# First attention layer with its queries in reverse order inside each block of 128, so that the bias table loads straight from its short form

## The reference, cut to what matters

```
q = rms_norm(proj[..., :o1].reshape(b, s, 16, 64), q_gain)
score = where(admissible, sum_h w[t,h] * relu(q_idx[t,h] . k_idx[s]), NEG)
_, idx = top_k(score, 64)
logits = einsum(q, k[idx]) * 64 ** -0.5 + rel_bias[t5_bucket(idx - t)]
p = softmax(where(valid, logits, NEG))
out = einsum(p, v[idx]) @ w_o
```

## Time and profile before

| | |
|---|---|
| median of 3 runs | 1142.5 us (1140.87 to 1145.25) |
| the profiled execution, its own time | 1142.08 us |
| its span, first to last instruction | 1140.3 us |
| mean granted TensorE clock | 0.994 of full |
| TensorE busy | 1114.7 us, 98% of the span |
| VectorE, ScalarE, GpSimd busy | 709.4, 583.4, 147.4 us |
| memory read, written | 191.90 MB, 6.37 MB |

### The profile page before, as it was taken

One profiled execution on the slowest core, in us unless ns is written; L12 is line 12 of the kernel. 1 busy time (PEld: TensorE's weight loads), 2 busy tenths in 40 slices (PEclk: granted clock), 3 DMA queues, 4 the chain that ended last, 5 costly groups with the idle time before them and its releaser, 6 DMA issues.

```text
span 1140.3 us, 17804 instructions
## 1 busy us (share of the span) xinstructions
PE 1114.7 (98%) x7045; PEld 987.8 (87%) x7045; DVE 709.4 (62%) x995; ACT 583.4 (51%) x767; POOL 147.4 (13%) x106
## 2 busy tenths in 40 slices
PE   8999999999999999999999999999999999999997
PEld 7768788888888888888888999898899989999996
DVE  5863665655668656556556877476587655554554
ACT  5583644444679554444455546445546346443443
POOL 3544200000266330000030000000000022000001
PEclk9999999999999999999999999999999999999999
DMA  7927465565342246555554655336554444655552
GB/s 224 313 70 180 160 221 185 185 191 190 112 138 104 74 137 227 190 185 184 188 180 162 209 152 182 114 122 238 177 166 132 165 150 152 220 180 194 189 172 89
DMA packets 138782, 193.96 MB, mean 170 GB/s; under 512 B 7147, under 2 KB 112840, under 8 KB 138716
## 3 DMA queue, kind: packets, MB, share of 16 engines
q1 hardware_dynamic: 126796, 181.92, 48.7%
q10 hardware_dynamic: 11312, 11.05, 3.6%
q0 software_dynamic: 608, 0.08, 0.1%
HBM read 191.90 MB, written 6.37 MB: 174 GB/s over the span
## 4 chain that ended last, share of the span: by engine, by line
PE 84%; DVE 6%; ACT 4%; DMA 2%; issue 2%; POOL 1%; SPq 0%; ACTq 0%; DVEq 0%
PE psum L546 20%; PE psum L547 20%; PE psum L548 20%; PE psum L707 11%; PE psum L708 5%; PE psum L635 2%; ACT arena L1553 2%; ACT whi L1567 1%; POOL wlo L1536 1%; DVE psum L2496 1%; DMA raw<-in_a_w_in 1%; DMA raw<-in_mlp_w_up 1%; PE psum L1265 1%; DVE wlo L2124 1%; DVE arena L2326 1%
## 5 line engine op out<-in xcount | busy, mean ns | idle before, releaser
L1567 ACT ACTIVATE whi<-raw 128x2048 fp32r<-128x2048 f32 (+2 forms) x174 | 325.8, 1874 | 260.8 <-PE psum L548 161.9
L2124 DVE TENSOR_TENSOR wlo<-raw,whi 128x2048 fp32r<-128x2048 f32 (+1 forms) x148 | 337.8, 2284 | 187.3 <-ACT whi L1567 186.4
L546 PE MATMUL psum<-xA,whi 128*128 128x256 f32 x840 | 240.1, 286 | 3.0 <-POOL wlo L1536 2.0
L547 PE MATMUL psum<-xA,whi 128*128 128x256 f32 x840 | 237.7, 283 | 0.0
L548 PE MATMUL psum<-xA,wlo 128*128 128x256 f32 x840 | 237.7, 283 | 0.0
L1536 POOL TENSOR_TENSOR wlo<-raw,whi 128x288 fp32r<-128x288 f32 (+3 forms) x57 | 117.3, 2083 | 803.6 <-ACT whi L1567 803.5
L707 PE MATMUL psum<-xA,whi 128*128 128x512 f32 x512 | 182.9, 400 | 0.8 <-DVE xA L2150 0.8
L546 PEld LDWEIGHTS psum<-xA,whi 128*128 128x128 f32 x840 | 160.7, 191 | 6.4 <-DVE wlo L2124 2.2
L547 PEld LDWEIGHTS psum<-xA,whi 128*128 128x128 f32 x840 | 160.7, 191 | 0.7
L548 PEld LDWEIGHTS psum<-xA,wlo 128*128 128x128 f32 x840 | 160.6, 191 | 0.1
L546 PE MATMUL psum<-whi,xC 128*128 128x512 f32 (+1 forms) x384 | 149.7, 390 | 1.1 <-DVE xC L2436 1.1
(11 more groups left out here) (272 smaller groups left out, 1344.0 us busy)
## 6 DMA issues: line engine op xcount, KB each, us to landing
raw<-in_w_in SPq DMA_DIRECT2D x42, 1024.0 KB, 5.0
raw<-in_mlp_w_up SPq DMA_DIRECT2D x32, 1024.0 KB, 5.5
raw<-in_mlp_w_down SPq DMA_DIRECT2D x32, 1024.0 KB, 4.9
raw<-in_w_gate SPq DMA_DIRECT2D x11, 1024.0 KB, 5.2
raw<-in_w_up SPq DMA_DIRECT2D x11, 1024.0 KB, 5.2
raw<-in_w_down SPq DMA_DIRECT2D x11, 1024.0 KB, 4.9
raw<-in_a_w_in SPq DMA_DIRECT2D x6, 1024.0 KB, 7.2
raw<-in_a_w_o SPq DMA_DIRECT2D x4, 1024.0 KB, 5.2
```

Source lines behind the costliest of these rows:

```text
L546: nc.tensor.matmul(out, lh, rh, start=start, stop=False, skip_group_check=skip)
L547: nc.tensor.matmul(out, lh, rl, start=False, stop=False, skip_group_check=skip)
L1567: nc.scalar.activation(whi[c % N_SPLIT][:, 0:n], raw[c % N_RAW][:, 0:n], ACT.Copy).then_inc(hi_sem, 1)
L2124: V.tensor_tensor(wlo[c % N_SPLIT][:, 0:n], raw[c % N_RAW][:, 0:n], f(whi[c % N_SPLIT][:, 0:n]), ALU.subtract).then_inc(lo_sem["dve"], 1)
```

## The change

The transposes of the queries use a matrix `flip` (the identity with its rows reversed) in the place of the identity, so that query 127 of a block comes first. Row r of the logits then is query 127 - r, and its bias is the line of the head from place r on: `A["toep"]` loads directly from `tab_a` with rows that start one value later each (`falling_rows`), and `skew_a` with its transfer is gone. The mask is brought into the same order by using the bf16 `flip` in its product, and the transposes of the attention's output use `flip` again, which restores the order. `flip` is loaded as one more constant, the first of the eleven behind `q0b`; its bf16 copy is made by DVE between the scores and the picking, behind a wait for all constants. TensorE waits for the constants ahead of the first query transposes. The third layer keeps its own path.

```
-        const_loads = [(relb[:, 16:40], t["rel_bias_2"]), ...
+        const_loads = [(flip[:, :], t["c_flip"]), (relb[:, 16:40], t["rel_bias_2"]), ...
...
-            def transposed(name, b, tiles):
+            def transposed(name, b, tiles, unit=ident):
...
-                    ins = nc.tensor.transpose(out[0:m, n * P:n * P + P], src, ident[:, :])
+                    ins = nc.tensor.transpose(out[0:m, n * P:n * P + P], src, unit[:, :])
...
                 pe.wait_ge(*done[f"A.qn{j}"])
+                if j == 0:
+                    pe.wait_ge(s_const, 16 * N_CONST)
                 for i, b in enumerate(banks):
                     transposed(f"A.qT{2 * j + i}", b, [A["q"][:, blk, k * P:k * P + P]
-                                                       for k in (4 * j + 2 * i, 4 * j + 2 * i + 1) for blk in range(NB)])
+                                                       for k in (4 * j + 2 * i, 4 * j + 2 * i + 1) for blk in range(NB)], flip)
...
-                        ins = nc.tensor.matmul(psum[:, logit_bank[h % 4], c0:c0 + w], ident_bf[:, :],
+                        ins = nc.tensor.matmul(psum[:, logit_bank[h % 4], c0:c0 + w], flip_bf[:, :],
                                                pick_mask[:, blk, 0:w], start=False, stop=True)
...
+            def falling_rows(tab, n):
+                return bass.AP(tab.ap().tensor, 0, [[1, P], [512, n], [1, SEQ]])
...
-            act.wait_ge(s_tab, 16)
-            shift_rows(tab_a, skew_a, 16)
...
-            act.wait_ge(s_skew, 16)
-            act.dma_start(A["toep"], skew_a.ap().rearrange("h p s -> p h s")).then_inc(s_toep_a, 16)
+            act.wait_ge(s_tab, 16)
+            act.dma_start(A["toep"], falling_rows(tab_a, 16)).then_inc(s_toep_a, 16)
...
-            run(V.tensor_copy(ident_bf[:, :], ident[:, :]), done["A.ident"])
+            run(V.tensor_copy(ident_bf[:, :], ident[:, :]))
...
+            dve.wait_ge(s_const, 16 * N_CONST)
+            run(V.tensor_copy(flip_bf[:, :], flip[:, :]), done["A.ident"])
```

More of the change, by code:

```diff
@@ L103, in shape_constants @@
         pick[h, h * P:(h + 1) * P] = 1.0
-    return {"c_ident": np.eye(P, dtype=np.float32), "c_one_a": one_a, "c_one_c": one_c, "c_off_c": off_c,
+    return {"c_ident": np.eye(P, dtype=np.float32), "c_flip": np.ascontiguousarray(np.eye(P, dtype=np.float32)[::-1]),
+            "c_one_a": one_a, "c_one_c": one_c, "c_off_c": off_c,
             "c_rope": rope, "c_turn": np.ascontiguousarray(turn), "c_chunk_mask": chunk_mask.astype(np.float32),
@@ L130, in program @@
         ident_bf = sb("ident_bf", [P, P], BF16)
+        flip = sb("flip", [P, P])
+        flip_bf = sb("flip_bf", [P, P], BF16)
         chunk_mask = sb("chunk_mask", [P, P], BF16)
@@ L143, in program @@
         tab_c = nc.dram_tensor("tab_c", (24, 512), F32, kind="Internal")
-        skew_a = nc.dram_tensor("skew_a", (16, P, SEQ), F32, kind="Internal")
         skew_c = nc.dram_tensor("skew_c", (24, P, SEQ), F32, kind="Internal")
@@ L492, in program @@
         tab_loads = [(relb[:, 0:16], t["rel_bias"]), (one_hot_a, t["c_one_a"])]
-        const_loads = [(relb[:, 16:40], t["rel_bias_2"]), (one_hot_c, t["c_one_c"]), (off_c, t["c_off_c"]),
+        const_loads = [(flip[:, :], t["c_flip"]), (relb[:, 16:40], t["rel_bias_2"]), (one_hot_c, t["c_one_c"]), (off_c, t["c_off_c"]),
                        (casts[:, 0, :], t["c_chunk_mask"]), (casts[:, 1, :], t["c_later"]),
@@ L774, in out_turned @@
                     transposed(f"{L}.oT{g}", g % 2, [S["o"][:, g, blk * 256 + i * P:blk * 256 + i * P + P]
-                                                     for i in range(2) for blk in range(NB)])
+                                                     for i in range(2) for blk in range(NB)], flip if L == "A" else ident)
                 def product(j, quarters):
@@ L1998, in _ @@
                     done[f"C.ya{k // 2}.hi"] if k % 2 else None, scale=vec(V_ML + k))
-            act.wait_ge(s_skew, 32)
+            act.wait_ge(s_skew, 16)
             for h in range(2):
```

## The result

The changed kernel takes 1149.97 us (median of 12 executions, 1147.18 to 1152.39) against 1144.95 us of the kernel before (12 executions, 1140.87 to 1150.53): a ratio of 1.0041, 95% interval 1.0021 to 1.0061. It is 5.0 us slower, and 1149.97 is outside the predicted range of 1139.2 to 1144.4. Of the 8.3 us between the forecast of 1141.7 and the result, 2.5 are in the kernel before, whose median over 12 executions is that much above the 1142.5 of its first three; the other 5.8 are a loss of 5.0 where a gain of 0.8 was forecast. The loss is 0.44%, so it still falls into the case "within 0.5%" that got 0.92, but its interval reaches beyond that. The profiled execution took 1151.51 us, with a span of 1149.7.

A forecast was written before the change was run, and what follows sets the result against it. TensorE, busy 98% of the span, bounds the kernel; only its waits can be won. Gains of 0.5 (q0b) and 0.6 (q1a), limited by POOL's scaling to 0.8, give 1141.3, or 1141.7 as median; range 1139.2 to 1144.4.

The forecast's parts named there:

- within 0.5%: Whole kernel: time changes by no more than 0.5% (5.7 us) either way; chance 0.92.
- the new copy of flip: DVE between scores and picking, near 39 us: costs 0.23 us, as the identity's cast did, plus 0.03 between instructions.
- What was late next: First query transposes at 55.89 wait for POOL's scaling, which hangs on DVE; gains there bring the total to 0.8 us.
- The wait for the constants: DVE ahead of flip's cast, about 39 us: priced at nothing, cover over 1 us; bound 1.5 us of wait.
- the signs that the forecast named for being wrong: Constants wait before DVE's cast, wo0 landing after 55, or a query transpose waiting over 0.5 us for POOL.
- The transfers: Without the shift, q1a lands 5.0 to 5.7 us after issue, not 11.1; bias load issued at 38.7, landing by 49.
- dear short form: Rival at the bias load: unaligned packets cost up to 102 ns, wo0 lands near 57.0, total 1143.7; chance 0.15.
- The 0.5 us for q0b: Second dot products at 34.22: q0b lands 0.55 us earlier without the shift, TensorE's wait shrinks from 1.22 to about 0.7.
- the forecast of 0.8: TensorE's total gain by the first query transposes at 55.89, taken from 0.55 to 0.9 us and carried to the end.
- more comes back: Rival at the attention's start: earlier wo0 pulls the first exponentials forward, up to 2 us gained, 1140.5; chance 0.12.
- Slower: Rival for the whole kernel: the bias load from the short form delays wo0, 1143.7; chance 0.15.
- the four cases: Whole kernel: forecast (0.3 to 1.5 us faster) 0.53, hidden anyway 0.2, more comes back 0.12, slow short form 0.15.

The follow-up runs named there:

- the old cast moved: Kernel before, with only the identity's bf16 cast moved from 29.7 us to ahead of the seventh picking turn, beside POOL's work; span 1141.3 us.
- the copy on ACT: Changed kernel with the bf16 copy of flip made by ACT behind the bias load's issue, not by DVE; ratio to before 0.9970, median 1140.98 us.
- the transfers alone: Kernel before without the first layer's shift, bias loaded directly from the short form, no flip (output differs); ratio to before 0.9982.
- flip alone: Kernel with flip copied by ACT, but the bias again through a written 2 MB table and a second load; ratio to before 1.0009.

## Why the prediction was wrong, by its own steps

**The step that failed** is in the sentence that begins "Against it goes the new copy of flip, 0.23 by the same cast of the identity". The row is right and was read without its surroundings. At 29.71 POOL was idle; at 38.5 it had just begun a subtraction, and that by my own sum (POOL from 38.7, DVE's cast "near 39"): the two stood side by side in the forecast, and nothing asked whether they can run together. The term measured 4.52 us. The trace of before showed the effect, in a row that I passed over. DVE's timeline has the same instruction twice, once while POOL's subtractions of 42.84 to 52.05 were under way, once without:

```profile
51.24 0.85 DVE L2302 TENSOR_SCALAR st<-st 128x16 f32<-128x16 f32 x1
...
62.82 0.17 DVE L2302 TENSOR_SCALAR st<-st 128x16 f32<-128x16 f32 x1
```

The first of them ends at 52.09, just behind POOL. The later profiles of before bear it out: in the second it took 1.30 us and ended at 52.91, with POOL's subtraction at 52.88; in the third, where POOL had ended at 53.75, it started at 55.21 and took 0.17. A blocked instruction has no bracket; it is only too long for its shape. The instructions of the picking are not long beside POOL (MAX8 0.29 us with and without it), which is why the picking never showed it.

```profile
51.61 1.30 DVE L2302 TENSOR_SCALAR st<-st 128x16 f32<-128x16 f32 x1
```

The Trainium skill says the same (SBUF — State Buffer, Who interferes with whom): copies, casts and tensor_scalar of DVE in their fast modes, and any DVE instruction with two inputs in SBUF against a GpSimd instruction that reads SBUF, share a port pair with GpSimd, and whoever comes first holds it for its whole instruction. The runs agree: 4.52 for the cast, 4.58 for the product of two SBUF inputs, 1.19 when POOL's instruction is a quarter as long, each ending within 0.2 us of POOL's instruction. That what is shared is a port, no run here can show; they show who waited, and how long. By that rule the term would have been the rest of POOL's 4.6 us.

**What was late next** was named rightly: POOL's scaling and the transposes behind it had 0.28 us of room. With a delay of 4 us in DVE the forecast's own structure gives the first half of the loss. The second half, 2.7 us, was in no step: in TensorE's wait of 3.91 us its clock fell to 1.2 GHz, and the transposes behind it took 1.97 us instead of 1.03.

**The wait for the constants** was priced at nothing, and it was nothing: DVE passed it with no wait. Of the signs that the forecast named for being wrong, the wait for constants did not come and wo0 landed in time; the third, a query transpose that waits over 0.5 us for POOL, did, with 3.91.

**The transfers** were right in mechanism, but not each gain has been seen. q1a landed 5.9 us after its issue, was copied at 36.30 with no wait, and the wait at its first product is gone. The bias load was issued at 36.30, at the start of that copy and not behind it (38.7), and landed at 47.1 (by 49). Its packets cost 1.082 x 16 x 2.4 / 821 = 51 ns each, in the range of 49 to 60 that I took, so the rival of a dear short form (beyond 87 ns) is out; wo0, issued at 42.94, landed 6.7 us later, near 49.6, and was copied at 55.04 and not before 54, because ACT waited for DVE.

The 0.5 us for q0b is not borne out. The changed kernel has its dot products 0.97 earlier than before (33.25 against 34.22), but its clock in the first 20 us was 1.00 and not 0.91. Where the clock there was the same, little is left: with the shift and 1.00, the kernel with the old cast moved has them at 33.42 and its key transposes at 45.98 (45.79 in the changed kernel); without the shift and at 0.91, the kernel with the copy on ACT has them at 34.08 and 34.53, around the 34.22 of before.

```profile
33.42 1.58 PE L871 MATMUL psum<-arena 64*128 64x128 f32 x16 [1.40 <-ACT arena L1553]
45.98 0.38 PE L635 MATMUL psum<-ident,arena 128*128 128x128 f32 x2
```

What holds is the part behind the dot products: the distance to the logits is 24.7 in all three profiles with neither shift nor cast, against 25.4 and 25.6 in the first two of before, a gain of 0.7 to 0.9. So the 0.84 at the logits with the cast off DVE (58.75; 0.40 in the second profile, 59.19) meets the forecast of 0.8 by way of this part, and some of the 1.2 where there is no flip (58.40) is the clock of the first 20 us.

In time the transfers alone gave 0.6 to 3.4 us, and with flip copied by ACT 1.7 to 5.3, which is above the 0.8. A likely reason, argued from few profiles and not shown, is that the first profile of before was one of its better executions: with the shift in flight q0b can also land 8.7 or 10.0 us after its issue, and TensorE's clock falls with the wait for it (0.82 of full at 34 to 36 us in the third profile of before, 0.83 at 36 to 46 us with flip alone). Over the three profiles of before and that of flip alone the logits start at 62.0 in the mean, over the three with neither shift nor cast at 58.8.

**The rival "more comes back"** named 2 us and looked for them in the attention. A gain of that size did come in the timed executions, but nothing shows it coming from there. That flip transposes and mask products are free holds: 8 of the transposes take 1.04 us with flip and 1.03 with the identity.

**Slower** had no rival with DVE's cast in it: the only slower case with a price was the dear short form, at 1143.7 and 0.15, and its cause did not occur. That the time moved by 5.0 us and still lies inside the 0.5% that got 0.92 is luck for that number, since none of the four cases under it is what happened.

## What to carry to other kernels

Before an instruction is priced by a row from elsewhere in the trace, look at what the neighbouring engine does at the new place: here a cast, a tensor_scalar and a product with both inputs in SBUF cost DVE the rest of the subtraction that POOL was executing, while MAX8 did not. Look for the same instruction with two durations in one profile: the longer one is a wait that no bracket shows. Small copies that must lie beside long POOL work go to ACT (0.29 us here, and the whole change then gains 0.3% instead of losing 0.4%); where they can't, cutting POOL's work into quarters cut the price to a quarter (1.19 us for 4.52), at 0.8 us more of POOL's time.

## What the runs showed of the hardware that I had not expected

A DVE instruction that loses to POOL waits for one POOL instruction and then gets in between two that are queued back to back (the cast ended at 42.99 with POOL's second subtraction to come, and after the first of eight pieces when they were short).

TensorE's clock was at 1.2 GHz after it had waited 3.91 us for POOL, until about 64 us, and cost 2.7 us on top of the wait; after a wait of 2.28 us (the old cast moved) it stayed at 2.4 GHz. The same stretch filled with idle products kept 2.4 GHz.

With a 2 MB transfer from memory to memory issued at the same time, a 1 MB load landed after 5.7, 5.9, 6.4, 8.7 and 10.0 us in five executions; without it after 5.2 to 6.2 in eight. Rows of 1 KB that each start 4 bytes further, from a 32 KB table, cost 51 ns a packet against 49 ns from an aligned table.
